# Half-height transpositions in pairs, into two neighbouring PSUM banks, in a two-block transformer kernel on one core

## The chip, the core and the metric

The kernel runs on one NeuronCore of a Trainium2 chip: TensorE (matrix products and transpositions), VectorE, ScalarE, GpSimd (POOL in the profile) and SyncE (SP), which issues the transfers. The metric is the device time of one execution in microseconds; lower is better.

## The reference, cut to what matters

Two blocks of two layers each over 256 positions of width 1024, batch 1, in float32. A layer of the first block projects x by `w_in`, runs three branches (retention with rotated queries and keys; chunk attention; differential attention with rotated queries and keys), merges them under gates, and ends in a feed-forward part:

```python
q = _rotary(q)                       # retention: 4 heads of 128
k = _rotary(k) * (dk ** -0.5)
...
q = _rotary(q) * (d ** -0.5)         # differential attention: 8 half heads of 64
k = _rotary(k)
...
merged = (g[:, :, 0] * jnp.einsum('bse,ed->bsd', o_a, w_branch_a[l])
          + g[:, :, 1] * jnp.einsum('bse,ed->bsd', o_b, w_branch_b[l])
          + g[:, :, 2] * jnp.einsum('bse,ed->bsd', o_c, w_branch_c[l]))
x = _layer_norm(DEEPNORM_ALPHA * x + mix, ln1_g[l], ln1_b[l])
u = jnp.einsum('bsd,df->bsf', x, w_ffn_in[l])
u_gate, u_up = jnp.split(u, 2, axis=-1)
ffn = jnp.einsum('bsf,fd->bsd', jax.nn.silu(u_gate) * u_up, w_ffn_out[l])
```

A layer of the second block is a feed-forward part, a mixer (convolution, gated MLP, sparse attention) and a second feed-forward part. So there are six feed-forward parts in all.

## The kernel before, in words

Every weight is brought in by SyncE in units of 128 x 2048 (`raw`), split by ScalarE into a rounded high part (`high`, L1857) and by VectorE into the low rest (`low`, L2096), both in `hl`. Each product is three matmuls, high by high, high by low, low by high (`mm3` L217 to L220, `mm3_onto` L223 to L227). TensorE needs the operand that is contracted with its positions along the free side, so results that come out with positions on the partitions are turned: `turn` (L1542) makes up to four 128 x 128 transpositions, one after the other, into one PSUM bank of 128 x 512; then ScalarE copies the bank out and, where high and low parts are wanted, VectorE subtracts.

The whole order is written out by a planner. `script` emits steps by name; each engine runs through the same list and does its part of every step in that order, so all five queues are in plan order. A step waits for semaphore counts of events that other engines' parts raise.

The eight PSUM banks are a ring, `PB` (class `Ring`, L186). `take` hands out the bank that was given back longest ago; `give` is called in the plan right after the steps that use the bank are added, and the next user's TensorE part waits for the event `free` that the last reader raises. Every bank carries a mark `dense`, set where its last use was a long projection or an accumulation. `take(True)` and `take(False)` prefer banks with or without that mark, plain `take()` goes by age alone (or by `spare`, where it is set). An accumulation holds its banks for long: a feed-forward part holds two from its third gate step and four from its fourth.

Steps that the change touches:
- `turn_split` (script L464, TensorE L1547, ScalarE L1860, VectorE L2099): the first x at the start (two steps of four blocks for each half of the rows; the steps that split the first weight unit, `lead`, stand between the two halves), the retention heads (`retention` L949, four blocks from a `tm` buffer), the differential attention (`da_attention` L1011, its `turn` makes two steps of four blocks one behind the other), and `gmlp`, which has a scale other than 1.
- `turn_copy` (TensorE L1554, ScalarE L1869): rotated queries and keys (`rot` L797, from an `rt` buffer, one step for each half of the rows, put off by one or two units), and the mask `gw` in `second_setup` L1089.
- `ffn_turn` (script L684, TensorE L1631, ScalarE L1918, VectorE L2183): in each feed-forward part (`ffn` L670) the first two hidden tiles come out with positions on the partitions and are turned, two blocks each. Both are put off by `P.later(1, ...)` and come out in one `tick`, one right behind the other.
- `ln_turn` (L1615), `weigh` (L1682) and the small transpositions of `stage_turn`, `pe_turn`, `gates_turn` and `cmp_gelu` (L1729 to L1782) are not touched.

Of the kernel before, what the change touches and what calls it, by code (L numbers as in the profile page):

```python
# [176 lines left out]
class Place:  # L177


    ring = None  # L180
# [5 lines left out]
class Ring:  # L186
# [5 lines left out]
    def take(self, dense=None):  # L192
# [259 lines left out]
def script(P):  # L452
# [11 lines left out]
    def turn_split(src, nk, dst, k0, src_events, before, i, out, scale=1.0, taken=()):  # L464

        for g in range(0, nk, 4):
            n = min(4, nk - g)
            b = PB.take()
            d = [dst[:, z, k0 + g:k0 + g + n, i * 128:(i + 1) * 128] for z in (0, 1)]
            last = g + 4 >= nk  # L470
            add("turn_split", b, [src[:, (g + k) * 128:(g + k + 1) * 128] for k in range(n)], src_events, taken if last else (),
                d, before, out(g, n), scale)
            PB.give(b)

# [322 lines left out]
    def rot(w, c0, nh, dh, dst, scale, name, before):  # L797
        yield from proj_n(w, c0)
        b = P.res
        for i in range(2):  # L800
            t1, t2 = RT.take(), TM.take()
            add("rotate", b[i], i, nh, dh, t1, t2)
            PB.give(b[i])
            TM.give(t2)

            def turn(i=i, t1=t1):
                tb = PB.take()
                add("turn_copy", tb, [t1.ap[:, k * 128:(k + 1) * 128] for k in range(4)], [t1.full], [t1.free],
                    dst[:, :, i * 128:(i + 1) * 128], before, [name + (i,)], scale)
                PB.give(tb)  # L810
                RT.give(t1)
            P.later(1 + i, turn)
        yield PART
# [60 lines left out]
    def first(l, o, now, nxt):  # L874
# [74 lines left out]
        def retention():  # L949
            def head(h):  # L950
# [10 lines left out]
                yield 1.3  # L961
                tb = PB.take()
                add("turn_split", tb, [tm.ap[:, i * 256 + c * 128:i * 256 + (c + 1) * 128] for c in range(2) for i in range(2)],
                    [tm.full], [tm.free], [O1[:, z, 2 * h:2 * h + 2, :] for z in (0, 1)], [P.o1_read], [("o1 ret", l)], 1.0)
                PB.give(tb)
                TM.give(tm)
# [122 lines left out]
    def second_setup(l, o):  # L1089
# [7 lines left out]
        for n, name in enumerate(("ck_w1_2", "cv_w1_2")):  # L1097
# [7 lines left out]
        yield 0.5  # L1105
        tb = PB.take()
        add("turn_copy", tb, [gw.ap[:, h * 128:(h + 1) * 128] for h in range(4)], [("gw masked", l)], [gw.free],
            m["wt"].rearrange("p (k t) -> p k t", k=4), [("wt read", l - 1)] if l else [("ca read", 1)], [("wt", l)], 1.0)
        PB.give(tb)
        RT.give(gw)  # L1110
# [310 lines left out]


class Signals:
    def __init__(self, sems, at):
# [107 lines left out]
def tensor_engine(e, P, steps, T, s):  # L1532
# [13 lines left out]

    def turn_split(b, blocks, events, taken, dst, before, out, scale):  # L1547
        e.wait_ge(*T["ident"])
        e.wait_ge(*T[b.before])
        for x in events:  # L1550
            e.wait_ge(*T[x])
        turn(b, blocks, *taken)

    def turn_copy(b, blocks, events, taken, dst, before, out, scale):  # L1554
        e.wait_ge(*T["ident"])
        e.wait_ge(*T[b.before])
        for x in events:
            e.wait_ge(*T[x])
        turn(b, blocks, *taken)

# [261 lines left out]
    def cmp_values(ob, l, et, first, last):  # L1822
# [4 lines left out]
        for c in range(2):  # L1827
# [3 lines left out]

    run(steps, dict(turn_split=turn_split, turn_copy=turn_copy, n_part=n_part, n_piece=n_piece, first_piece=first_piece, t_part=t_part,
                    ln_turn=ln_turn, out_piece=out_piece, ffn_turn=ffn_turn, ffn_down=ffn_down, score_pair=score_pair, score_parts=score_parts,
# [5 lines left out]
def scalar_engine(e, P, steps, T, s):  # L1839
# [19 lines left out]

    def turn_split(b, blocks, events, taken, dst, before, out, scale):  # L1860
        e.wait_ge(*T[b.full])
# [6 lines left out]

    def turn_copy(b, blocks, events, taken, dst, before, out, scale):  # L1869
        e.wait_ge(*T[b.full])  # L1870
        for x in before:
            e.wait_ge(*T[x])
        n = len(blocks)
        e.activation(dst, b.ap[:, 0:n * 128].rearrange("p (k t) -> p k t", k=n), ACT.Copy, scale=scale).then_inc(done.up(b.free, *out), 1)

# [42 lines left out]
    def ffn_turn(tb, tm, h, before, out):  # L1918
        e.wait_ge(*T[tb.full])
        e.wait_ge(*T[before])  # L1920
        e.activation(h[:, 0], tb.ap[:, 0:256], ACT.Copy).then_inc(done.up(("high",) + out), 1)

# [101 lines left out]
    run(steps, dict(start=start, lead_high=lead_high, high=high, turn_split=turn_split, o_split=turn_split, turn_copy=turn_copy, copy=copy, q_parts=q_parts, k_parts=k_parts, silu_gate=silu_gate, ln_split=ln_split,  # L2024
                    seed=seed, ffn_gate=ffn_gate, ffn_turn=ffn_turn, ffn_split=ffn_split, soft=soft, biased=biased,
# [44 lines left out]
def vector_engine(e, P, steps, T, s):  # L2070
# [27 lines left out]

    def turn_split(b, blocks, events, taken, dst, before, out, scale):  # L2099
# [367 lines left out]
    def cmp_turn(l, i, er, tb, et):  # L2467
# [4 lines left out]

    run(steps, dict(start=start, masks=masks, low=low, turn_split=turn_split, o_split=turn_split, scale=scale, rotate=rotate, silu_gate=silu_gate, ln_stats=ln_stats,
                    ln_norm=ln_norm, ln_split=ln_split, ln_last=ln_last, ffn_gate=ffn_gate, ffn_turn=ffn_turn,
# [87 lines left out]
```

## Time and profile before

| | |
|---|---|
| runs, median (lowest to highest) | 1980.91 us (1980.73 to 1981.51) |
| the profiled execution | 1980.39 us |
| its span in the trace | 1978.6 us |
| TensorE matmul, busy | 1966.6 us (99%), 13888 instructions |
| TensorE weight load, busy | 1801.2 us (91%) |
| VectorE, busy | 1248.4 us (63%) |
| ScalarE, busy | 911.8 us (46%) |
| GpSimd, busy | 98.6 us (5%) |
| TensorE's granted clock | 0.999 of full speed on average |

PE is TensorE's matmul, PEld its weight load, DVE VectorE, ACT ScalarE. A row of the time line is a run of like instructions: start in us from the start of the span, length, engine, line of the code, operation, output and input, `rows*columns` of the weights, shape of the moving operand, and how many. Matmuls overlap in the records, for each one's length holds its latency; what one costs is the distance from its start to the next one's. All transpositions of `turn` stand under L1544, with their data as the weights and the unit matrix (`cst`) moving.

### The profile page before, as it was taken

The page shows a single profiled execution, that of the slowest core. Times are in us where ns is not written, and L with a number is a line of the kernel's source. Part 1 is how long each engine was busy: PE and PEld are TensorE (multiplying, and loading weights), DVE is VectorE, ACT ScalarE, POOL GpSimd, SP SyncE. Part 2 cuts the span into 40 slices and gives each one's busy share as a digit, 9 for nine tenths or more (in the row PEclk, how much of TensorE's full clock was granted, in tenths as well). Part 3 has the DMA queues.
Part 4 walks back from the last instruction along what each step waited for, and adds up shares of the span by engine and source line. Part 5 has one row for each costly group of instructions (what it writes and reads, how often), then busy time and mean ns, then how long its engine had stood idle before and what let it go on. Part 6 is the DMA issues. An engine that isn't in the chain of part 4 may idle for free.

```text
span 1978.6 us, 31903 instructions
## 1 busy us (share of the span) xinstructions
PE 1966.6 (99%) x13888; PEld 1801.2 (91%) x13888; DVE 1248.4 (63%) x1759; ACT 911.8 (46%) x1217; POOL 98.6 (5%) x84
## 2 busy tenths in 40 slices
PE   8999999999999999999999999999999999999998
PEld 7889999999888999999999989899999998989997
DVE  6566666565756666655565567765556556776555
ACT  4445544444445555444354445544444444555442
POOL 0000001000100000100010020010010002001000
PEclk9999999999999999999999999999999999999999
DMA  7544566676454355696666656478666664646663
GB/s 282 189 143 140 180 204 197 198 209 192 170 170 149 133 187 192 196 262 180 184 209 185 186 168 171 108 201 258 183 179 204 186 188 150 192 114 197 186 186 106
DMA packets 421446, 361.85 MB, mean 183 GB/s; under 512 B 29425, under 2 KB 361529, under 8 KB 421305
## 3 DMA queue, kind: packets, MB, share of 16 engines
q1 hardware_dynamic: 421160, 359.74, 59.6%
q8 instruction: 109, 1.79, 0.4%
q14 instruction: 33, 0.26, 0.0%
q10 hardware_dynamic: 144, 0.07, 0.0%
HBM read 358.72 MB, written 1.05 MB: 182 GB/s over the span
## 4 chain that ended last, share of the span: by engine, by line
PE 99%; DVE 0%; DMA 0%; DVEq 0%; ACT 0%; issue 0%
PE ps L218 23%; PE ps L220 23%; PE ps L219 23%; PE ps L225 8%; PE ps L227 8%; PE ps L226 8%; PE ps L1544 3%; PE ps L1707 1%; PE ps L1655 1%; PE ps L1672 1%; PE ps L1745 0%; PE ps L1696 0%; PE ps L1813 0%; DMA cst<-in_const 0%; PE ps L1829 0%; PE ps L1723 0%
## 5 line engine op out<-in xcount | busy, mean ns | idle before, releaser
L2096 DVE TENSOR_TENSOR hl<-raw,hl 128x1024 fp32r<-128x1024 f32 (+2 forms) x535 | 722.2, 1383 | 382.0 <-ACT hl L1857 381.4
L218 PE MATMUL ps<-xt,hl 128*128 128x256 f32 (+1 forms) x2672 | 754.6, 282 | 0.0
L219 PE MATMUL ps<-xt,hl 128*128 128x256 f32 (+1 forms) x2672 | 746.2, 279 | 0.0
L220 PE MATMUL ps<-xt,hl 128*128 128x256 f32 (+1 forms) x2672 | 745.8, 279 | 0.0
L1857 ACT ACTIVATE hl<-raw 128x2048 fp32r<-128x2048 f32 (+1 forms) x338 | 613.7, 1824 | 218.6 <-PE ps L227 156.8
L218 PEld LDWEIGHTS ps<-xt,hl 128*128 128x128 f32 (+1 forms) x2672 | 500.9, 187 | 6.5 <-issue 3.1
L219 PEld LDWEIGHTS ps<-xt,hl 128*128 128x128 f32 (+1 forms) x2672 | 501.0, 188 | 3.1
L220 PEld LDWEIGHTS ps<-xt,hl 128*128 128x128 f32 (+1 forms) x2672 | 500.8, 187 | 0.2
L225 PE MATMUL ps<-hl,o 128*128 128x512 f32 x656 | 261.4, 398 | 0.0
L227 PE MATMUL ps<-hl,o 128*128 128x512 f32 x656 | 259.0, 395 | 0.0
L226 PE MATMUL ps<-hl,o 128*128 128x512 f32 x656 | 258.8, 394 | 0.0
L218 PE MATMUL ps<-hl,xt 128*128 128x512 f32 (+1 forms) x576 | 206.9, 359 | 0.5 <-DVE hl L2096 0.5
L1916 ACT ACTIVATE th<-ps 128x256 f32<-128x256 f32 x132 | 50.6, 384 | 328.8 <-PE ps L220 328.8
L220 PE MATMUL ps<-hl,xt 128*128 128x512 f32 (+1 forms) x576 | 202.1, 351 | 0.0
L219 PE MATMUL ps<-hl,xt 128*128 128x512 f32 (+1 forms) x576 | 202.1, 351 | 0.0
L227 PEld LDWEIGHTS ps<-hl,o 128*128 128x128 f32 x656 | 123.5, 188 | 28.9
L225 PEld LDWEIGHTS ps<-hl,o 128*128 128x128 f32 x656 | 123.5, 188 | 26.7 <-issue 0.8
L226 PEld LDWEIGHTS ps<-hl,o 128*128 128x128 f32 x656 | 123.7, 189 | 25.3
L218 PEld LDWEIGHTS ps<-hl,xt 128*128 128x128 f32 x576 | 108.4, 188 | 18.7 <-issue 1.7
L220 PEld LDWEIGHTS ps<-hl,xt 128*128 128x128 f32 x576 | 108.3, 188 | 15.9
L219 PEld LDWEIGHTS ps<-hl,xt 128*128 128x128 f32 x576 | 108.5, 188 | 14.5
L2179 DVE SCALAR_TENSOR_TENSOR tm<-th,ps 128x256 f32<-128x256 f32 x132 | 55.4, 420 | 98.9 <-ACT th L1916 94.8
(206 smaller groups left out, 1572.3 us busy)
## 6 DMA issues: line engine op xcount, KB each, us to landing
raw<-in_w_in SPq DMA_DIRECT2D x83, 1024.0 KB, 5.0
raw<-in_w_ffn_in SPq DMA_DIRECT2D x88, 512.0 KB, 5.1
raw<-in_ffn_gate SPq DMA_DIRECT2D x88, 512.0 KB, 3.9
raw<-in_ffn_up SPq DMA_DIRECT2D x88, 512.0 KB, 5.2
raw<-in_ffn_down SPq DMA_DIRECT2D x44, 1024.0 KB, 5.1
raw<-in_w_ffn_out SPq DMA_DIRECT2D x22, 1024.0 KB, 5.0
raw<-in_w_out SPq DMA_DIRECT2D x24, 512.0 KB, 4.6
raw<-in_w_branch_a SPq DMA_DIRECT2D x8, 1024.0 KB, 5.0
```

What stands on the lines that cost most here:

```text
L218: e.matmul(out, l[0], r[0], start=start, stop=False)
L219: e.matmul(out, l[0], r[1], start=False, stop=False)
L220: return e.matmul(out, l[1], r[0], start=False, stop=stop)
L225: e.matmul(out, l[0], r[0], start=False, stop=True, skip_group_check=True)
L226: e.matmul(out, l[0], r[1], start=False, stop=True, skip_group_check=True)
L227: return e.matmul(out, l[1], r[0], start=False, stop=True, skip_group_check=True)
L1544: ins = e.transpose(b.ap[:, k * 128:(k + 1) * 128], x, ident)
L1655: ins = e.matmul(b.ap[:, n * K:(n + 1) * K], qs[n][hh], ks[n][hh], start=n == 0, stop=mask is None and n == 1)
L1857: e.activation(m["hl"][:, k % NHL, 0, c], m["raw"][:, k % NRAW, c], ACT.Copy).then_inc(s.high.up(*([("high", k, h)] if parts == 2 else [(" ...
L1916: e.activation(tha, ga, ACT.Tanh, scale=0.5).then_inc(done.up(th.full), 1)
L2096: e.tensor_tensor(lo[:, c], m["raw"][:, k % NRAW, 0:n][:, c], hi[:, c].bitcast(F), ALU.subtract).then_inc(s.low.up(("low", k), *([("low", ...
L2179: e.scalar_tensor_tensor(tma, tha, 1.0, ga, ALU.add, ALU.mult).then_inc(done.up(th.free), 1)
```

## The change

Where a step turned blocks into one bank, it now takes two banks with neighbouring numbers (`Pair`, `neighbours`), and each block becomes two transpositions of 64 rows: the upper half's into the first bank, the lower half's into the second, 64 columns each. ScalarE and VectorE read both banks in one instruction through a view of four dimensions (`two_halves`). `turn_split` with scale 1, `turn_copy` and `ffn_turn` are changed; `turn_split` with another scale goes on as `turn_whole`.

```diff
+    def neighbours(self, dense=None):
+
+        dense = self.spare if dense is None else dense
+        age = {slot: n for n, slot in enumerate(self.order)}
+        pairs = [(dense is not None and (self.dense[x] != dense) + (self.dense[x + 1] != dense), max(age[x], age[x + 1]), x) for x in age if x + 1 in age]
+        x = min(pairs)[2]
+        return [self.at(slot) for slot in (x, x + 1)]
+
+    def at(self, slot):
+        self.order.remove(slot)
+        self.n += 1
+        u = Use(self, slot, self.n, self.latest[slot])
+        self.latest[slot] = u.free
+        return u
...
+class Pair:
+
+    def __init__(self, ring, psum, kind=False):
+        self.uses = ring.neighbours(kind)
+        a = self.uses[0].slot
+        self.ap = psum[:, a:a + 2, :]
+        self.before = [u.before for u in self.uses]
+        self.full, self.free = [u.full for u in self.uses], [u.free for u in self.uses]
...
-            b = PB.take()
+            b = Pair(PB, m["psum"]) if scale == 1.0 else PB.take()
...
-            PB.give(b)
+            PB.give(*(b.uses if scale == 1.0 else [b]))
...
                 def turn():
-                    tb = PB.take()
+                    tb = Pair(PB, m["psum"])
                     add("ffn_turn", tb, tm, h, free, ("ht", f, j))
-                    PB.give(tb)
+                    PB.give(*tb.uses)
...
+def two_halves(pair, dst, k0=0):
+
+    src = pair.ap[:, :, 64 * k0:64 * (k0 + dst.shape[1])].rearrange("p h (k t) -> p h k t", t=64)
+    return src, dst.rearrange("p k (h t) -> p h k t", h=2)
...
+    def turn_halves(pair, blocks, *events):
+        for k, x in enumerate(blocks):
+            for h in range(2):
+                rows = slice(64 * h, 64 * h + 64)
+                ins = e.transpose(pair.ap[:, h, k * 64:(k + 1) * 64], x[rows], ident[rows, rows])
+        ins.then_inc(done.up(*pair.full, *events), 1)
...
     def ffn_turn(tb, tm, h, before, out):
-        e.wait_ge(*T[tb.before])
+        for x in tb.before:
+            e.wait_ge(*T[x])
         e.wait_ge(*T[tm.full])
-        turn(tb, [tm.ap[:, i * 128:(i + 1) * 128] for i in (0, 1)], tm.free)
+        turn_halves(tb, [tm.ap[:, i * 128:(i + 1) * 128] for i in (0, 1)], tm.free)
...
     def ffn_turn(tb, tm, h, before, out):
         e.wait_ge(*T[("high",) + out])
-        e.tensor_tensor(h[:, 1], tb.ap[:, 0:256], h[:, 0].bitcast(F), ALU.subtract).then_inc(done.up(out, tb.free), 1)
+        (src, hi), (_, lo) = (two_halves(tb, blocks_of(h[:, z])) for z in (0, 1))
+        e.tensor_tensor(lo, src, hi.bitcast(F), ALU.subtract).then_inc(done.up(out, *tb.free), 1)
```

The other users of `turn_split` and `turn_copy` change in the same way: `Pair` in place of `PB.take()`, all of `tb.uses` given back, `turn_halves` in place of `turn`, `two_halves` in ScalarE's and VectorE's parts.

## Rows read from the trace of the kernel before

**Rows 1.** The page, part 1 (busy) and part 4 (chain by engine).
```profile
PE 1966.6 (99%) x13888; PEld 1801.2 (91%) x13888; DVE 1248.4 (63%) x1759; ACT 911.8 (46%) x1217; POOL 98.6 (5%) x84
...
PE 99%; DVE 0%; DMA 0%; DVEq 0%; ACT 0%; issue 0%
```

**Rows 2.** All waits of PE: who waited for whom, us in total, times, longest.
```profile
PE ps L1544 <- DMA cst<-in_const: 4.7, 1, 4.7
PE ps L218 <- DVE hl L2096: 0.5, 1, 0.5
```

**Rows 3.** Groups of instructions by line and form, L1544 on PE.
```profile
L1544 PE MATMUL ps<-cst,xs 128*128 128x128 f32 x160 | 22.8, 289 | 4.7 <-DMA cst<-in_const 4.7
...
L1544 PE MATMUL ps<-cst,rt 128*128 128x128 f32 x72 | 10.8, 272 | 0.0
L1544 PE MATMUL ps<-cst,tm 128*128 128x128 f32 x72 | 10.4, 272 | 0.0
```

**Rows 4.** Time line of PE, 91.6 to 92.8 us.
```profile
91.82 0.28 PE L219 MATMUL ps<-xt,hl 128*128 128x256 f32 x1
91.94 0.28 PE L220 MATMUL ps<-xt,hl 128*128 128x256 f32 x1
92.05 0.60 PE L1544 MATMUL ps<-cst,tm 128*128 128x128 f32 x4
...
92.61 0.28 PE L219 MATMUL ps<-xt,hl 128*128 128x256 f32 x1
```

**Rows 5.** Time line of PEld from 1220.3 us.
```profile
1220.52 0.14 PEld L1753 LDWEIGHTS ps<-cst,tm 30*128 30x128 f32 x2
```

**Rows 6.** Time line of PEld from 1246 us.
```profile
1246.57 0.97 PEld L1813 LDWEIGHTS ps<-small,q 64*128 64x128 f32 x16 [0.17 <-ACT th L1880]
```

**Rows 7.** Time line of PEld, 896.3 to 897.4 us.
```profile
896.71 0.13 PEld L1729 LDWEIGHTS ps<-cst,stage 12*128 12x128 f32 x1
896.77 0.14 PEld L1735 LDWEIGHTS ps<-cst,stage 32*128 32x128 f32 x1
896.83 0.14 PEld L1736 LDWEIGHTS ps<-cst,stage 32*128 32x128 f32 x1
```

**Rows 8.** Time line of PE, the same stretch.
```profile
896.51 0.27 PE L220 MATMUL ps<-xt,hl 128*128 128x256 f32 x1
...
897.35 0.39 PE L226 MATMUL ps<-hl,o 128*128 128x512 f32 x1
```

**Rows 9.** Time line of PEld, the start.
```profile
4.74 3.27 PEld L1544 LDWEIGHTS ps<-cst,xs 128*128 128x128 f32 x16 [4.74 <-DMA cst<-in_const]
```

**Rows 10.** Time line of DVE, 331 to 334.3 us, the first feed-forward part.
```profile
329.03 4.49 DVE L2096 TENSOR_TENSOR hl<-raw,hl 128x2048 fp32r<-128x2048 f32 x2 [1.97 <-ACT hl L1857]
333.44 0.75 DVE L2185 TENSOR_TENSOR o<-ps,o 128x256 fp32r<-128x256 f32 x2
```

**Rows 11.** Time line of PE, the same stretch.
```profile
331.23 0.60 PE L1544 MATMUL ps<-cst,tm 128*128 128x128 f32 x4
```

**Rows 12.** Time line of DVE, 237 to 243 us.
```profile
239.84 0.69 DVE L2107 TENSOR_TENSOR o<-ps,o 128x512 fp32r<-128x512 f32 x1 [0.31 <-ACT o L1867]
```

**Rows 13.** Time line of PE, 238.1 to 239.3 us.
```profile
238.29 1.03 PE L1544 MATMUL ps<-cst,tm 128*128 128x128 f32 x8
```

**Rows 14.** Time line of DVE, 109.6 to 113 us.
```profile
111.98 1.28 DVE L2107 TENSOR_TENSOR o<-ps,o 128x512 fp32r<-128x512 f32 x2
```

**Rows 15.** Time line of PE, 111.1 to 111.7 us.
```profile
111.28 0.60 PE L1544 MATMUL ps<-cst,tm 128*128 128x128 f32 x4
```

**Rows 16.** Time line of DVE, 157.9 to 160 us.
```profile
157.91 0.41 DVE L2121 TENSOR_TENSOR tm<-ps,cst 128x256 f32<-128x256 f32 x1
...
158.97 0.68 DVE L2212 COPY et<-ps 128x512 f32<-128x512 f32 x1
```

**Rows 17.** Time line of PE, 157.7 to 158.4 us.
```profile
157.91 0.60 PE L1544 MATMUL ps<-cst,rt 128*128 128x128 f32 x4
```

**Rows 18.** Busy time by stretch: us, PE, PEld, DVE, ACT, POOL, granted clock, DMA share, GB/s.
```profile
12.00:1974.00 1962.00, 1959.83 (x13860) 1795.42 (x13859) 1241.35 (x1747) 905.70 (x1208) 98.42 (x80) 1.00 0.60 182
```

More of the change, by code:

```diff
@@ L467, in turn_split @@
             n = min(4, nk - g)
-            b = PB.take()
+            b = Pair(PB, m["psum"]) if scale == 1.0 else PB.take()
             d = [dst[:, z, k0 + g:k0 + g + n, i * 128:(i + 1) * 128] for z in (0, 1)]
             last = g + 4 >= nk
-            add("turn_split", b, [src[:, (g + k) * 128:(g + k + 1) * 128] for k in range(n)], src_events, taken if last else (),
+            add("turn_split" if scale == 1.0 else "turn_whole", b, [src[:, (g + k) * 128:(g + k + 1) * 128] for k in range(n)], src_events, taken if last else (),
                 d, before, out(g, n), scale)
-            PB.give(b)
+            PB.give(*(b.uses if scale == 1.0 else [b]))
     def n_parts(w, r, c0, src, src_events, banks, first, last, after=()):
@@ L806, in turn @@
             def turn(i=i, t1=t1):
-                tb = PB.take()
+                tb = Pair(PB, m["psum"])
                 add("turn_copy", tb, [t1.ap[:, k * 128:(k + 1) * 128] for k in range(4)], [t1.full], [t1.free],
                     dst[:, :, i * 128:(i + 1) * 128], before, [name + (i,)], scale)
-                PB.give(tb)
+                PB.give(*tb.uses)
                 RT.give(t1)
@@ L961, in head @@
                 yield 1.3
-                tb = PB.take()
+                tb = Pair(PB, m["psum"])
                 add("turn_split", tb, [tm.ap[:, i * 256 + c * 128:i * 256 + (c + 1) * 128] for c in range(2) for i in range(2)],
                     [tm.full], [tm.free], [O1[:, z, 2 * h:2 * h + 2, :] for z in (0, 1)], [P.o1_read], [("o1 ret", l)], 1.0)
-                PB.give(tb)
+                PB.give(*tb.uses)
                 TM.give(tm)
@@ L1105, in second_setup @@
         yield 0.5
-        tb = PB.take()
+        tb = Pair(PB, m["psum"])
         add("turn_copy", tb, [gw.ap[:, h * 128:(h + 1) * 128] for h in range(4)], [("gw masked", l)], [gw.free],
             m["wt"].rearrange("p (k t) -> p k t", k=4), [("wt read", l - 1)] if l else [("ca read", 1)], [("wt", l)], 1.0)
-        PB.give(tb)
+        PB.give(*tb.uses)
         RT.give(gw)
@@ L1420, in quarter, with blocks_of @@
     return banks[c // 2].ap[:, 256 * (c % 2):256 * (c % 2) + 256].rearrange("p (k t) -> p k t", k=2)
+def two_halves(pair, dst, k0=0):
+    src = pair.ap[:, :, 64 * k0:64 * (k0 + dst.shape[1])].rearrange("p h (k t) -> p h k t", t=64)
+    return src, dst.rearrange("p k (h t) -> p h k t", h=2)
+def blocks_of(ap):
+    if len(ap.shape) == 2:
+        return ap.rearrange("p (k t) -> p k t", t=128)
+    return ap if ap.shape[2] == 128 else ap.rearrange("p k (m t) -> p (k m) t", t=128)
 class Signals:
@@ L1545, in turn, with turn_split, turn_whole @@
         ins.then_inc(done.up(b.full, *events), 1)
-    def turn_split(b, blocks, events, taken, dst, before, out, scale):
+    def turn_halves(pair, blocks, *events):
[4 more added lines that the diff above has]
+        ins.then_inc(done.up(*pair.full, *events), 1)
+    def turn_split(pair, blocks, events, taken, dst, before, out, scale):
         e.wait_ge(*T["ident"])
+        for x in pair.before + events:
+            e.wait_ge(*T[x])
+        turn_halves(pair, blocks, *taken)
+    def turn_whole(b, blocks, events, taken, dst, before, out, scale):
         e.wait_ge(*T[b.before])
@@ L1552, in turn_split, with turn_copy @@
         turn(b, blocks, *taken)
-    def turn_copy(b, blocks, events, taken, dst, before, out, scale):
+    def turn_copy(pair, blocks, events, taken, dst, before, out, scale):
         e.wait_ge(*T["ident"])
-        e.wait_ge(*T[b.before])
-        for x in events:
+        for x in pair.before + events:
             e.wait_ge(*T[x])
-        turn(b, blocks, *taken)
+        turn_halves(pair, blocks, *taken)
     def n_part(g, b, src, r, k0, i, src_events, first, last, after, seeded=False):
@@ L1631, in ffn_turn @@
     def ffn_turn(tb, tm, h, before, out):
-        e.wait_ge(*T[tb.before])
+        for x in tb.before:
+            e.wait_ge(*T[x])
         e.wait_ge(*T[tm.full])
-        turn(tb, [tm.ap[:, i * 128:(i + 1) * 128] for i in (0, 1)], tm.free)
+        turn_halves(tb, [tm.ap[:, i * 128:(i + 1) * 128] for i in (0, 1)], tm.free)
     def ffn_down(g, b, i, c, slots, h_events, events):
@@ L1830, in cmp_values @@
         ins.then_inc(done.up(ob.full, et.free, ("vb read", l), ("win read", l)), 1)
-    run(steps, dict(turn_split=turn_split, turn_copy=turn_copy, n_part=n_part, n_piece=n_piece, first_piece=first_piece, t_part=t_part,
+    run(steps, dict(turn_split=turn_split, turn_whole=turn_whole, turn_copy=turn_copy, n_part=n_part, n_piece=n_piece, first_piece=first_piece, t_part=t_part,
                     ln_turn=ln_turn, out_piece=out_piece, ffn_turn=ffn_turn, ffn_down=ffn_down, score_pair=score_pair, score_parts=score_parts,
@@ L1858, in high, with turn_split, o_split @@
             s.high.up(*([("high", k, h)] if parts == 2 else [("high", k, 0), ("high", k, 1)])), 1)
-    def turn_split(b, blocks, events, taken, dst, before, out, scale):
+    def turn_split(pair, blocks, events, taken, dst, before, out, scale):
+        e.wait_ge(*T[pair.full[1]])
+        for x in before:
+            e.wait_ge(*T[x])
+        src, d = two_halves(pair, blocks_of(dst[0]))
+        e.activation(d, src, ACT.Copy, scale=scale).then_inc(done.up(("split high", pair.full[1])), 1)
+    def o_split(b, blocks, events, taken, dst, before, out, scale):
         e.wait_ge(*T[b.full])
@@ L1867, in turn_split, with turn_copy @@
         e.activation(dst[0], src, ACT.Copy, scale=scale).then_inc(done.up(("split high", b.full)), 1)
-    def turn_copy(b, blocks, events, taken, dst, before, out, scale):
-        e.wait_ge(*T[b.full])
+    def turn_copy(pair, blocks, events, taken, dst, before, out, scale):
+        e.wait_ge(*T[pair.full[1]])
         for x in before:
             e.wait_ge(*T[x])
-        n = len(blocks)
-        e.activation(dst, b.ap[:, 0:n * 128].rearrange("p (k t) -> p k t", k=n), ACT.Copy, scale=scale).then_inc(done.up(b.free, *out), 1)
+        src, d = two_halves(pair, dst)
+        e.activation(d, src, ACT.Copy, scale=scale).then_inc(done.up(*pair.free, *out), 1)
     def copy(b, src, dst, scale, before, out):
@@ L1918, in ffn_turn @@
     def ffn_turn(tb, tm, h, before, out):
-        e.wait_ge(*T[tb.full])
+        e.wait_ge(*T[tb.full[1]])
         e.wait_ge(*T[before])
-        e.activation(h[:, 0], tb.ap[:, 0:256], ACT.Copy).then_inc(done.up(("high",) + out), 1)
+        src, d = two_halves(tb, blocks_of(h[:, 0]))
+        e.activation(d, src, ACT.Copy).then_inc(done.up(("high",) + out), 1)
     def ffn_split(tm, h, before, out):
@@ L2022, in cmp_exp @@
         e.activation(er.ap[:, 0:120], er.ap[:, 0:120], ACT.Exp).then_inc(done.up(("cmp exp", l, i)), 1)
-    run(steps, dict(start=start, lead_high=lead_high, high=high, turn_split=turn_split, o_split=turn_split, turn_copy=turn_copy, copy=copy, q_parts=q_parts, k_parts=k_parts, silu_gate=silu_gate, ln_split=ln_split,
+    run(steps, dict(start=start, lead_high=lead_high, high=high, turn_split=turn_split, o_split=o_split, turn_whole=o_split, turn_copy=turn_copy, copy=copy, q_parts=q_parts, k_parts=k_parts, silu_gate=silu_gate, ln_split=ln_split,
                     seed=seed, ffn_gate=ffn_gate, ffn_turn=ffn_turn, ffn_split=ffn_split, soft=soft, biased=biased,
@@ L2097, in low, with turn_split, o_split @@
             s.low.up(("low", k), *([("low", k, h)] if parts > 1 else [("low", k, 0), ("low", k, 1)])), 1)
-    def turn_split(b, blocks, events, taken, dst, before, out, scale):
+    def turn_split(pair, blocks, events, taken, dst, before, out, scale):
+        (src, hi), (_, lo) = (two_halves(pair, blocks_of(x)) for x in dst)
+        e.wait_ge(*T["split high", pair.full[1]])
+        low_part((hi, lo), src, scale).then_inc(done.up(*pair.free, *out), 1)
+    def o_split(b, blocks, events, taken, dst, before, out, scale):
         n = len(blocks) * 128
@@ L2471, in cmp_turn @@
                         ALU.mult).then_inc(done.up(et.full, tb.free), 1)
-    run(steps, dict(start=start, masks=masks, low=low, turn_split=turn_split, o_split=turn_split, scale=scale, rotate=rotate, silu_gate=silu_gate, ln_stats=ln_stats,
+    run(steps, dict(start=start, masks=masks, low=low, turn_split=turn_split, o_split=o_split, turn_whole=o_split, scale=scale, rotate=rotate, silu_gate=silu_gate, ln_stats=ln_stats,
                     ln_norm=ln_norm, ln_split=ln_split, ln_last=ln_last, ffn_gate=ffn_gate, ffn_turn=ffn_turn,
```

## The prediction

> **What bounds the kernel now.** I read the page's busy shares and its chain first: TensorE is busy 99% of the span and is the whole chain [rows 1]. Then its waits: in the whole span it stands still for the constant at the start and for 0.5 us after that, and for nothing else [rows 2]. So TensorE's own stream is the time. Whatever is added to it or taken from it moves the end one for one, and no later wait is there to absorb it. VectorE (63%) and ScalarE (46%) matter only where TensorE is made to wait for them. The span is 1978.6 us, the profiled execution 1980.39 us, the median of the runs 1980.91 us: 0.5 us lies between the last two, and I carry it over.
>
> **What is removed.** The diff touches 160 of the 480 transpositions at L1544: 16 of the first x, 72 from `rt`, 72 from `tm` [rows 3] (of the 160 from `xs`, 16 are the first x; the rest are `ln_turn`, which stays). The mean of 272 ns for one is latency; the cost is the pitch. Four of them cost this: the last matmul before starts at 91.94, the second one after at 92.61, which is 0.67 us; without them these two steps would be 2 x 0.117 = 0.23 (the pitch of L218 to L220 beside them). So a group of four costs 0.44 us, or 0.11 per block, with next to nothing at the edges [rows 4].
>
> **What is added on TensorE.** Each block becomes two instructions of 64 rows with 64 moving columns, in two banks. The trace has no 64-row transposition with 64 columns; the nearest rows are the small ones.
> Do the halves run beside each other? Two weight loads of 30-row transpositions at rows 0 and 32 stand in one row of 0.14 us, where one alone takes 0.13 [rows 5]; and 16 loads of 64 rows in alternating halves take 0.97 us, so a pair takes about 0.11 [rows 6]. I take it that pairs do overlap.
> How close do pairs follow? A transposition's weight load of 128 columns follows the one before by 0.06 us (896.71, 896.77, 896.83) [rows 7]; 64 moving columns are half of the 0.11 that 128 take, 0.05. So a pair costs 0.06, against 0.11 before. The bound above is the 0.11 of [rows 6], whose loads aren't transpositions; below it is the 0.05 of the moving columns. I take 0.06, since those rows are the same operation.
> What does leaving and entering cost? The three small transpositions of [rows 7] stand in a stream of full-height matmuls: from the last one before (896.51) to the second after (897.35) is 0.84 us, where 0.12 + 0.23 = 0.35 would do [rows 8]. They cost 0.49, of which 3 x 0.06 is their own. So 0.31 us is the price of going to fewer rows and coming back; the first load starts 0.20 after the matmul before it, where it otherwise runs ahead, and so does the load after the last. With 32 more moving columns in the last pair (0.03), four pairs cost 0.31 + 0.24 + 0.03 = 0.58 us against 0.44: 0.14 **more**. Two such groups in a row (eight blocks) cost 0.82 against 0.88.
> The Trainium skill speaks of this edge (TensorEngine Tiling (Array Packing), Key Properties): a change of the tiling mode drains TensorE, a change of tile alone doesn't. The trace agrees, with the 0.31 above. The skill also says (TensorE: Matmul & The Clock Gate, LDWEIGHTS) that a load costs by its columns, P/1.2, whatever its rows; for 128 columns that estimate is 107 ns a load, which [rows 7] contradict for transpositions with 0.06. What the higher pitch would do is worked out from [rows 6] among the rivals.
>
> **The sum of that.** The 160 blocks stand in 46 steps: 4 at the start, 16 in `rot`, 2 for `gw`, 8 in `retention`, 4 in `da_attention` (two directly after two), 12 in `ffn` (two blocks each, two steps in a row, so six runs of four). Two of the 16 in `rot` are followed by 64-row scores, whose own drain they take over: four pairs save 0.19 there, and nothing is added. So 14 + 2 + 8 + 6 = 30 runs x 0.14 = +4.2, two runs of eight x -0.06 = -0.1, two x -0.19 = -0.4: **+3.7 us**. At the start the sixteen have a pitch of 0.20 (3.27 us) [rows 9], and half the moving columns should halve it; the first L218 after them waits for VectorE [rows 2], which is fed by the first eight: the first x is split earlier by up to 8 x 0.1 = 0.8, and the lead copies on ScalarE stand behind that. **-0.6 us**, between 0 (if the lead's loads are late) and -0.9.
>
> **Banks, the larger term.** A pair takes two neighbours, and `neighbours` ranks by how many of the two were last used densely, before it looks at age. Banks that a pair gave back count as not dense. I stepped the list of free banks through the order of the takes and gives, with the new rule. In `ffn`, at the first of the two steps, five banks are free (before the first one 7, 5, 4, 6, 2, of which 7, 6 and 2 dense); 4 and 5 are taken, given back in the plan at once, and the second step finds 7, 6, 2, 4, 5 and takes **4 and 5 again**, for it is the only neighbouring pair without a dense bank. So the second transposition waits until VectorE has read the first result. Before, it had another bank. The same holds in all six `ffn`, and it is a wait of TensorE, with every projection queued behind it.
> Its length is in the trace of before. VectorE works through two `low` of L2096 until 333.52 and then does L2185, two in 0.75, so the first is done at about 333.86 [rows 10]. TensorE starts the second pair of blocks 0.22 after 331.23, at 331.45 [rows 11]. The wait is 2.4 us, six times: **14.5 us**.
> The same list gives the same clash elsewhere, in each of the two first layers: `da_attention`, second step, wants the banks that L2107 leaves at 239.84 + 0.69 = 240.53, when TensorE is at 238.29 + 0.43 = 238.72, 1.8 us [rows 12, 13]. `retention`, last head: free after the first L2107, 111.98 + 0.68, wanted at 111.28: 1.4 us [rows 14, 15]. `rot` for the keys of `da`, first half: its bank 6 was last a `weigh`, which L2212 reads until 158.97 + 0.68 = 159.65; wanted at 157.91: 1.7 us [rows 16, 17]. One `retention` head more comes 0.2 too early. Together 5.1 a layer, **10.2 us**. All other pairs find banks that have been free for over half a microsecond, and no other taker falls short. Each of the 14 waits ends in a load that nothing hides, and a semaphore: some 0.1 each (0.03 to 0.2), **+1.4 us**.
> Reading two banks in runs of 64 costs the readers nothing that I can see: L2121 reads 128 x 256 out of PSUM with a stride in 0.41, as L2185 does without [rows 10, 16]. If it cost 0.1, 14 waits would be 1.4 us longer. The ScalarE side has slack, it works ahead of VectorE. Nothing is moved on SP's or GpSimd's queue.
>
> Sum on the profiled execution: 1980.4 + 3.7 - 0.6 + 24.7 + 1.4 = 2009.6; plus 0.5 for the median: **2010 us**.
>
> **The rivals.**
> 1. Loads don't go faster for transpositions of half height, or the halves don't overlap: the pair costs 0.11, as in [rows 6]. 114 pairs (all but the first of each of the 46 steps) x 0.05 = +5.7, and the start gains nothing: 2016. For it: those are the only alternating 64-row loads with few columns. Against: [rows 7]. The page's rule for loads, above, would come to this rival. Chance 0.12.
> 2. The clock falls. Granted is 1.00, the 2.4 GHz level, from 12 to 1974 us [rows 18], and TensorE never stood still for over 0.5 us there. The first sixteen, right after 4.74 us of nothing, go at 0.20 instead of 0.11 a block [rows 9], as at the 1.2 GHz level. If the eight waits of 1.8 us and more did the same and cost some 2 us each: +16, 2026. Against: they are half as long. Chance 0.08. The Trainium skill (TensorE: Matmul & The Clock Gate, Part 1) lets the clock drop only after longer idling than these waits; no row of before shows that.
> 3. The banks come free in time (VectorE reads the pair ahead of its `low`, or the plan's order differs from my stepping): only the edges remain, 1980.9 + 3.7 - 0.6 = 1984. Against: the queues are in plan order and the `low` stands first. Chance 0.05.
> 4. **Faster**: going to 64 rows costs nothing for transpositions, and the banks are free. 144 blocks x 0.05 = -7.2, with -0.6: 1973. It decides at 0.17 us per edge pair; below that four pairs win. Against: 0.31 in [rows 8], themselves transpositions. Chance 0.02.
> That the diff doesn't do what it says I see no way for: 160 instructions more on TensorE are certain.
>
> **How the numbers follow.** The forecast has 0.71: its own range is 2004 to 2015 (pitch 0.05 to 0.07, waits shorter by what TensorE loses ahead of them, the start 0 to -0.9, readers +1.4). A last 0.02 goes to waits that are over half hidden, 1990 to 2000. With rivals 1 and half of 2 the range is 2000 to 2022. A measurement of this kernel can tell about 0.2% (4 us) from no change. Faster by that: rival 4 and nothing else, 0.02. Within: rival 3 (1984 is +0.16%), 0.05. Slower: 0.93.
>
> **What would show it.** In the profile after: 14048 matmuls; waits of TensorE's transpositions for VectorE's L2185-successor, six of about 2.4 us, in the chain too; eight more of 0.2 to 1.8; pairs of transpositions with starts a few ns apart and 0.06 from pair to pair; 0.2 before the first and about 0.2 after the last; the clock still 1.00. If TensorE's waits stay under 2 us in total, the stepping of the banks is wrong. If single waits exceed 3 us, ScalarE or VectorE fell behind as well.

## The result and the profile after

| | before | after |
|---|---|---|
| runs, median (lowest to highest) | 1981.11 us (1980.73 to 1981.58) | 2018.21 us (2013.75 to 2019.49) |
| the profiled execution | 1980.39 us | 2019.49 us |
| its span in the trace | 1978.6 us | 2017.7 us |
| mean granted clock of that execution | 0.999 | 0.994 |

The change made the kernel slower: ratio 1.0183, 95% interval 1.0172 to 1.0194, five runs each (the 1980.91 us of the forecast was the median of the first three of before). The forecast was 2010 us, with a range of 2000 to 2022. It said +29 us; the medians are 37.1 us apart, the spans of the two profiled executions 39.1 us. The direction and the banks were seen rightly; about 10 us came from something that the forecast had set at nothing.

The busy line and the chain by engine (the page of after), which answer to [rows 1]:

```profile
PE 1981.8 (98%) x14048; PEld 1806.0 (90%) x14048; DVE 1251.3 (62%) x1759; ACT 914.6 (45%) x1217; POOL 98.6 (5%) x84
...
PE 92%; DVE 5%; ACT 2%; issue 0%; DMA 0%; POOL 0%; DVEq 0%
```

VectorE was 0% of the chain and is now 5%. All waits of TensorE in after, the view of [rows 2] (who waited for whom, us in total, times, longest). L1588 is the half-height transposition; L2248 is `ffn_turn` on VectorE, L2169 the subtraction of `turn_split`, L2275 VectorE's copy in `weigh`, L2153 `low`:

```profile
PE ps L1588 <- DVE o L2248: 13.8, 6, 2.3
PE ps L1588 <- DVE o L2169: 5.8, 4, 1.7
PE ps L1588 <- DMA xs<-in_x: 5.0, 1, 5.0
PE ps L1588 <- DVE et L2275: 3.3, 2, 1.7
PE ps L233 <- DVE hl L2153: 1.1, 1, 1.1
```

Six waits of 2.3 us in the feed-forward parts and six of 1.13 to 1.75 elsewhere are 22.9 us. What one of the six is made of stands in the chain of after between 338 and 344 us (start, length, what):

```profile
338.17 4.49 DVE hl L2153 x2
342.67 0.34 DVE o L2248
...
343.06 0.35 PE ps L1588 x4
```

It is the forecast's story: two `low` of 2.2 us each stand ahead of the step that reads the bank, and TensorE stands until that is read. The same place on TensorE in after (start, length, engine, line, operation, tiles, weights, moving operand, how many):

```profile
340.20 0.27 PE L235 MATMUL ps<-xt,hl 128*128 128x256 f32 x1
340.41 0.34 PE L1588 MATMUL ps<-cst,tm 64*128 64x64 f32 x4
343.06 0.35 PE L1588 MATMUL ps<-cst,tm 64*128 64x64 f32 x4 [2.31 <-DVE o L2248]
343.34 0.58 PE L233 MATMUL ps<-xt,hl 128*128 128x256 f32 x1
...
344.57 0.41 PE L235 MATMUL ps<-xt,hl 128*128 128x256 f32 x1
344.78 0.41 PE L233 MATMUL ps<-xt,hl 128*128 128x256 f32 x1
```

Before the wait such products follow each other by 0.117 us, after it by 0.21. That is the part which the forecast lacked. Stretches of after with the granted clock (from:to and its length, busy time with instructions of PE, PEld, DVE, ACT and POOL, then the clock, the DMA share and GB/s):

```profile
247.70:251.10 3.40, 3.40 (x19) 3.40 (x18) 2.33 (x3) 1.44 (x1) 0.00 (x0) 0.50 0.59 228
343.30:346.70 3.40, 3.40 (x20) 3.36 (x17) 1.60 (x4) 2.25 (x6) 0.00 (x0) 0.51 1.08 341
843.35:846.80 3.45, 1.14 (x11) 1.08 (x12) 2.60 (x4) 1.04 (x3) 0.00 (x0) 1.00 0.61 178
1036.20:1039.60 3.40, 3.10 (x16) 2.99 (x17) 1.84 (x5) 1.59 (x5) 0.00 (x0) 0.50 1.16 337
```

A clock of 0.5 is the 1.2 GHz level. Three more such stretches follow, at 1343.4, 1534.5 and 1841.7 us. So the clock fell six times, five times at a wait of 2.3 us and once at one of 1.75. It didn't fall at a fixed distance from the wait: at 1036.2 us TensorE still stood for another 0.3 us (the wait ended at 1036.49), at 343.3 the wait had ended 0.2 us before, and at 247.7 it had ended 1.4 us before, with 1.4 us of work in between. The third line shows the 2.3 us wait (843.35 to 845.66 us) that it did not fall after. In before it stays at the 2.4 GHz level from 12 to 1974 us [rows 18]. One fall costs what is lost at half speed: 3.4 us x (1 - 0.117 / 0.213) = 1.5 us; the later matmuls of after, held against the same matmuls of before, move by 1.55 to 1.65 us over each stretch. Six falls are some 9.7 us.

The whole move of that execution then adds up. Of 39.1 us, 22.9 are the waits, 9.7 the falls, 1.2 the start (below), and 5.3 are left for the edges and restarts at 46 steps.

### The profile page after: what moved, and what is told of

Same layout as the page of the kernel before. It is cut to its first block, busy times and chain, and to the rows that moved or that the text cites. A ratio compares the mean times of both kernels' runs of the same rounds, so it can differ in the third digit from the quotient of the medians.

```text
span 2017.7 us, 32221 instructions
## 1 busy us (share of the span) xinstructions
PE 1981.8 (98%) x14048; PEld 1806.0 (90%) x14048; DVE 1251.3 (62%) x1759; ACT 914.6 (45%) x1217; POOL 98.6 (5%) x84
## 4 chain that ended last, share of the span: by engine, by line
PE 92%; DVE 5%; ACT 2%; issue 0%; DMA 0%; POOL 0%; DVEq 0%
PE ps L233 22%; PE ps L235 21%; PE ps L234 21%; PE ps L240 8%; PE ps L242 8%; PE ps L241 8%; DVE hl L2153 2%; PE ps L1581 2%; ACT hl L1906 1%; PE ps L1756 1%; PE ps L1588 1%; PE ps L1721 1%; PE ps L1704 0%; DVE small L2264 0%; PE ps L1794 0%
## 5 line engine op out<-in xcount | busy, mean ns | idle before, releaser
L2153 DVE TENSOR_TENSOR hl<-raw,hl 128x1024 fp32r<-128x1024 f32 (+2 forms) x535 | 723.4, 1384 | 399.1 <-ACT hl L1906 398.5
```

Source lines behind the costliest of these rows:

```text
L2153: e.tensor_tensor(lo[:, c], m["raw"][:, k % NRAW, 0:n][:, c], hi[:, c].bitcast(F), ALU.subtract).then_inc(s.low.up(("low", k), *([("low", ...
```

## The experiments

All ran for one core, each with runs of the kernel before on the same chip: its median there was 1980.81 us for the first four and 1980.78 us for the last four. Two theories stood at the outset. **Theory A**: the time went to the waits for banks, and the clock fell because TensorE stood still; the halves themselves cost only their edges. **Theory B**: the halves or the two-bank reads cost more themselves, and bring the falls about.

**1. Feed-forward turns share a pair.** Both turns of a feed-forward part write different columns of one pair, and the readers wait for both:

```diff
-                    tb = Pair(PB, m["psum"])
+                    if j == 0:
+                        shared.append(Pair(PB, m["psum"]))
+                    tb = shared[0].part(2 * j)
...
-                    PB.give(*tb.uses)
+                    if j == 1:
+                        PB.give(*tb.uses)
```

> The changed kernel, but in each feed-forward part the two turns use different columns of one pair of banks, so that the second no longer waits for the first to be read (readers wait for both). Theory (waits for banks, and clock falls that follow the waits): six waits of 2.5 us and five clock falls of 1.7 us go: 2018.2 - 15.0 - 8.5 = 1995 us, with at most one stretch at half clock left, after the differential attention. Rival (the clock falls because of the half-height transpositions themselves): only the waits go, 2003 us, and five or more half-clock stretches stay.

Measured: 1996.65 us (1994.77 to 1997.14), ratio 1.0078, interval 1.0063 to 1.0093. The waits of the feed-forward parts are gone from TensorE's list, the others are as they were (waits of this kernel, then its one stretch at the lower clock):

```profile
PE ps L1602 <- DVE o L2183: 5.8, 4, 1.7
PE ps L1602 <- DVE et L2289: 3.3, 2, 1.6
```
```profile
746.80:750.30 3.50, 3.50 (x19) 3.50 (x18) 2.44 (x3) 1.25 (x1) 0.00 (x0) 0.51 0.52 202
```

The medians of this kernel and of after are 21.6 us apart: 13.8 us of waits and five falls fewer (8 us) make 21.8. The falls left with the waits, while the halves stayed.

**2. No pair that was just given back.** Experiment 1, and the search for a pair looks first at whether a bank is one of the last two given back:

```diff
+        late = self.order[-2:]
-        pairs = [(dense is not None and (self.dense[x] != dense) + (self.dense[x + 1] != dense), ...
+        pairs = [((x in late) + (x + 1 in late), (self.dense[x] != dense) + (self.dense[x + 1] != dense), ...
```

> As e1, and the pair is chosen by a rule that avoids the two banks given back last, so that nearly no pair has to wait (0.8 us in all by the free list). What is left is the price of the edges, 0.13 to 0.14 us a group as read from the two traces (3.4 us in all), the start (1.2 us), and no clock falls: 1986.5 us. Rival (half-height transpositions lower the clock): 1992 or more, with half-clock stretches. Rival (the edges were really part of the waits): 1982.

Measured: 1986.54 us (1986.06 to 1987.4), ratio 1.0029, interval 1.0018 to 1.004. TensorE's waits, with the one for the constant left out:

```profile
...
PE ps L235 <- DVE hl L2168: 1.2, 1, 1.2
PE ps L1603 <- DVE tm L2198: 0.7, 2, 0.4
```

The clock falls nowhere in TensorE's work. Against the trace of before the end moves by 5.9 us: 0.8 at the start, 0.9 in the two small waits with their restarts, and 4.2 at the edges. That is the price of the halves themselves, and they have no gain to set against it. The other 31.7 us of the change (1986.54 to 2018.21) came from the choice of banks.

**3. After's pairs, but full height.** The order of takes and gives stays; the transposition is that of before and writes the first bank only, and the readers read that one alone:

```diff
-            for h in range(2):
-                rows = slice(64 * h, 64 * h + 64)
-                ins = e.transpose(pair.ap[:, h, k * 64:(k + 1) * 64], x[rows], ident[rows, rows])
+            ins = e.transpose(pair.ap[:, 0, k * 128:(k + 1) * 128], x, ident)
...
```

> The changed kernel's pairs of banks and its waits, but each block is turned whole, 128 rows, into the first bank of the pair; the second bank is held and unused. Theory: waits (22.9 us) and clock falls stay, edges (3.4 us) and the slow start (1.2 us) go: 2013.5 us. Rival (the clock falls because of the half-height transpositions): no half-clock stretches, 2004 us.

Measured: 2012.81 us (2009.29 to 2014.85), ratio 1.0159, interval 1.0144 to 1.0174. The waits of the feed-forward parts, and one of this kernel's four stretches at the lower clock (the others start at 1339.0, 1530.2 and 1837.4 us):

```profile
PE ps L1585 <- DVE o L2245: 14.0, 6, 2.4
```
```profile
1031.80:1035.20 3.40, 3.34 (x16) 3.35 (x17) 1.60 (x5) 1.62 (x5) 0.00 (x0) 0.50 1.15 340
```

Theory B falls: with no half-height instruction and no two-bank read in the kernel, it is 32 us slower than before, and the clock falls as in after. Together with experiment 2 this shows that the wait brings the fall. The halves' own price comes out smaller here than in experiment 2: after ends 4.7 us later than this kernel in the traces, 3.2 us of that are its two falls more, and 1.5 us are left. At the eight groups in `rot` that no wait follows after takes 0.14 to 0.16 us longer; where a wait stands, part of the edge comes off the wait (in `retention` 1.13 us in after against 1.26 and 1.27 here).

**4. Halves not alternated.** Experiment 2, with all upper halves of a group first and then all lower ones:

```diff
-        for k, x in enumerate(blocks):
-            for h in range(2):
+        for h in range(2):
+            for k, x in enumerate(blocks):
```

> As e2, but a group first turns the upper halves of all its blocks and then the lower ones, so that neighbours in the stream use the same 64 rows. Theory (halves overlap only when they alternate; a pair costs 0.06 us, one after the other 0.12): 160 x 0.06 = 9.6 us over e2, 1996 us. Rival (TensorE overlaps them in any order, or never did): the time of e2.

Measured: 1986.97 us (1986.33 to 1987.55), ratio 1.0031, interval 1.0019 to 1.0042: experiment 2's time. My theory, that the halves overlap only when one of each follows the other, fell. The first `rt` group of after on TensorE, and then the same group of this kernel:

```profile
26.77 0.39 PE L235 MATMUL ps<-hl,xt 128*128 128x512 f32 x1
27.08 0.46 PE L1588 MATMUL ps<-cst,rt 64*128 64x64 f32 x8
...
27.81 0.39 PE L234 MATMUL ps<-hl,xt 128*128 128x512 f32 x1
```
```profile
26.89 0.40 PE L237 MATMUL ps<-hl,xt 128*128 128x512 f32 x1
27.22 0.47 PE L1603 MATMUL ps<-cst,rt 64*128 64x64 f32 x8
...
27.96 0.39 PE L236 MATMUL ps<-hl,xt 128*128 128x512 f32 x1
```

From the last product before the group to the second one after it (the first is not shown) there are 1.04 us in after and 1.07 here. Within the group the loads of a pair start 3 ns apart in after and 12 ns apart here, and the pairs follow each other by 0.06 us in both, although here four loads of the upper rows were issued ahead of the first of the lower rows.

**5. The start at full height.** Experiment 2, with the first x turned as in before:

```diff
+            halved = scale == 1.0 and dst is not XT
-            b = Pair(PB, m["psum"]) if scale == 1.0 else PB.take()
+            b = Pair(PB, m["psum"]) if halved else PB.take()
...
```

> As e2, but the first x is turned whole, 128 rows into one bank, as before; half-height pairs everywhere else. Theory (the start loses because the clock comes up late in these runs whatever the transpositions are; the halves themselves save 0.4 us there, by the first product's start in e2 and e3): 1986.9 us, 0.4 over e2. Rival (it is the half-height transpositions at the start that hold the clock down): 1985.3 us, and the clock up by 8.1 us as in the kernel before.

Measured: 1988.69 us (1986.86 to 1989.5), ratio 1.0038, interval 1.0024 to 1.0051. The time doesn't answer what the run was made for. The start takes other banks, the list stands in another order from there on, and one clash came back (a wait of TensorE, and the clock just after it):

```profile
PE ps L1604 <- DVE o L2186: 1.8, 1, 1.8
```
```profile
243.60:247.00 3.40, 3.40 (x18) 3.40 (x18) 2.30 (x4) 1.76 (x1) 0.00 (x0) 0.50 0.68 264
```

Without that wait and fall (1.8 + 1.6 us) it would be near 1985.3, the rival's number. That is worked out, not measured, and the hit is partly luck: against the trace of experiment 2 the start gives 0.56 us, and a small wait that is absent here 0.48. The trace of the start does speak for the rival. The products of 512 columns go at the full pace from the first one on, which starts at 9.06 us:

```profile
9.37 0.39 PE L236 MATMUL ps<-hl,xt 128*128 128x512 f32 x1
9.60 0.39 PE L237 MATMUL ps<-hl,xt 128*128 128x512 f32 x1
```

The run also shows how brittle a fixed list is: four steps changed at the start, and a wait appears 240 us later.

**6. The upper rows twice.** Experiment 2, with both transpositions of a pair reading rows 0 to 63. The lower halves of the turned blocks are left out:

```diff
-                ins = e.transpose(pair.ap[:, h, k * 64:(k + 1) * 64], x[rows], ident[rows, rows])
+                ins = e.transpose(pair.ap[:, h, k * 64:(k + 1) * 64], x[0:64], ident[0:64, 0:64])
```

> As e2, but both transpositions of a pair read rows 0 to 63, so nothing in a group uses the other half of the rows (the lower halves are left out; the output isn't the reference's). Theory (two streams overlap because they use different rows, in whatever order they are issued): loads follow at 0.06 us each, a pair costs 0.12, 160 x 0.06 = 9.6 us over e2: 1996 us. Rival (TensorE issues any two of them together): the time of e2.

Measured: 1993.87 us (1993.34 to 1994.79), ratio 1.0065, interval 1.0052 to 1.0079. The same group on TensorE in this kernel:

```profile
28.35 0.40 PE L237 MATMUL ps<-hl,xt 128*128 128x512 f32 x1
28.67 0.71 PE L1603 MATMUL ps<-cst,rt 64*128 64x64 f32 x8
...
29.66 0.40 PE L236 MATMUL ps<-hl,xt 128*128 128x512 f32 x1
```

1.31 us instead of 1.04, so 0.07 more per pair than in after; against experiment 2 a group of four takes 0.24 to 0.25 us more, 0.06 per pair. The overlap is real and needs different rows: with it a pair costs 0.06 us, without it 0.12. The 36 groups' worth of blocks behind the start times 0.24 is 8.6 us, less 0.9 for experiment 2's two small waits, which are absent here: 7.7. The two medians are 7.3 us apart. The sum is no closer than a microsecond or two, for the starts of the two profiled runs differ by 1.95 us besides.

**7. Only where eight blocks stand together.** The kernel before, with half-height pairs in one place, the groups of eight in the sparse attention of the second block (`weigh`), which the change had left alone. One pair of banks holds all eight:

```diff
+        if P.both and PB.spare is None:
+            pair = Pair(PB, m["psum"])
+            for n in range(2):
+                er, et = ers[n], ET.take()
+                add("weigh_pair", pair, n, [er.ap[:, k * 128:k * 128 + 128] for k in range(4)], er, ...)
...
+            PB.give(*pair.uses)
```

> The kernel before, with half-height pairs only in eight groups of eight blocks in the second block's sparse attention (turned weights), where one pair of banks holds both results and no bank is taken besides. Theory (a group costs 0.34 + 0.06 a block against 0.11 a block; two groups are followed by 64-row scores whose drain is there anyway): 6 x -0.06 and 2 x -0.4 = -1.1 us, 1980.0 us, no new waits. Rival (the two readers' wait for both halves reaches the values): +0.5 us a group, 1985.

Measured: 1979.84 us (1979.52 to 1980.52, 11 runs), ratio 0.9995, interval 0.9986 to 1.0004. One of its two groups that 64-row scores follow, in before and then in this kernel:

```profile
1245.48 0.28 PE L220 MATMUL ps<-xt,hl 128*128 128x256 f32 x1
1245.61 1.03 PE L1544 MATMUL ps<-cst,er 128*128 128x128 f32 x8
1246.57 1.07 PE L1813 MATMUL ps<-small,q 64*128 64x15 f32 x16
1247.57 0.38 PE L218 MATMUL ps<-xt,hl 128*128 128x256 f32 x1
```
```profile
1245.71 0.28 PE L238 MATMUL ps<-xt,hl 128*128 128x256 f32 x1
1245.92 0.71 PE L1721 MATMUL ps<-cst,er 64*128 64x64 f32 x16
1246.46 1.02 PE L1850 MATMUL ps<-small,q 64*128 64x15 f32 x16
1247.41 0.38 PE L236 MATMUL ps<-xt,hl 128*128 128x256 f32 x1
```

From the product before to the product after there are 2.09 us in before and 1.70 here. So where the work behind is at 64 rows anyway, eight pairs do gain, 0.38 to 0.39 us at each of two groups, and the other six gain 0.03 to 0.04 each. That sums to 1 us in 1980, which the interval can't tell from nothing. No wait was added.

**8. The kernel before again**, for a second trace of its start.

> The kernel before, unchanged, for a second profile of its start. Theory (when the clock comes up at the start varies from run to run): up anywhere from 8 to 13 us, span between 1978.5 and 1980. Rival (8.1 us belongs to the kernel before): 8.1 us again.

Measured: 1981.29 us, span 1979.5. Its start on TensorE, and then that of after (the profile's clock column doesn't show this first stretch, so it is read from the distances of the products):

```profile
4.93 3.65 PE L1544 MATMUL ps<-cst,xs 128*128 128x128 f32 x16 [4.93 <-DMA xs<-in_x]
8.97 0.76 PE L218 MATMUL ps<-hl,xt 128*128 128x512 f32 x1 [0.40 <-DVE hl L2096]
...
10.67 0.40 PE L219 MATMUL ps<-hl,xt 128*128 128x512 f32 x1
10.91 0.40 PE L220 MATMUL ps<-hl,xt 128*128 128x512 f32 x1
```
```profile
5.04 2.34 PE L1588 MATMUL ps<-cst,xs 64*128 64x64 f32 x32 [5.04 <-DMA xs<-in_x]
8.43 0.77 PE L233 MATMUL ps<-hl,xt 128*128 128x512 f32 x1 [1.06 <-DVE hl L2153]
...
11.98 0.48 PE L235 MATMUL ps<-hl,xt 128*128 128x512 f32 x1
12.30 0.40 PE L233 MATMUL ps<-hl,xt 128*128 128x512 f32 x1
```

Products of 512 columns follow by 0.43 us at first and by 0.23 later. The change of pace came at about 10.5 us here and at 8.1 in the first trace of before. With the first x turned at full height it came at 11.2, 8.1 and 9.5 us in experiments 3, 5 and 7; with halves at the start at 12.2 in after and at 13.0, 11.5, 12.6 and 14.9 in experiments 1, 2, 4 and 6. So it varies by 3 us within each kind, and the two kinds don't overlap: the five starts at full height lie between 8.1 and 11.2, the five with halves between 11.5 and 14.9, with one trace of each run.

## Why the prediction was right, and where it was wrong

**Banks.** Right, and by the steps given. The stepping of the free list named six clashes in the feed-forward parts and three larger ones in each of the two first layers; the waits came there and nowhere else. The six were put at 2.4 us and measured 2.3. `da_attention` 1.8, measured 1.75; `rot` 1.7, measured 1.65; `retention` 1.4, measured 1.13. The two of 0.2 us did not show. In sum 24.7 us forecast, 22.9 measured: TensorE came a little later to each, and that took the difference off the wait.

**Edges and restarts.** 3.7 + 1.4 = 5.1 us forecast, 5.3 left over in the sum above. A group of four takes 1.04 us in after, where before took 0.91 (25.59 to 26.50): +0.13, with 0.14 forecast from three small transpositions of 12 and 32 rows [rows 7, 8]. The split between the two terms is less exact than their sum: experiment 2 puts the edges alone at 4.2 us, which leaves 1.1 for the restarts. The reader of two banks takes 0.42 us (L2248), as with one (L2185), so that it costs nothing was right too. A feed-forward part moves TensorE by 2.65 us in all, wait, restart and edge; the steps gave 2.4 + 0.1 + 0.14 = 2.64.

**Overlap.** Right in the number, 0.06 us per pair; experiment 6 shows that it comes from the different rows. Rival 1 (0.11) is out. So is the Trainium skill's rule that it leaned on (TensorE: Matmul & The Clock Gate, LDWEIGHTS): with 107 ns a load, an estimate by that rule, loads on the same rows could not follow each other by 0.06 us, and in experiment 6 they do (eight loads of L1603 in 0.58 us, each 0.14 long).

**The start.** The step that put it at -0.6 us failed, and it measured +1.2 (profiled execution of after against that of before). The first product did start 0.38 us earlier, within the forecast's 0 to -0.9. What the step didn't see is that the products behind it run at half pace until the clock rises, and that this came at 12.2 us in after, behind 3.7 us of products, where in before it came ahead of the first product. Part of the +1.2 is chance: experiment 3, at full height, has +1.2 as well. At the product that starts at 20 us in before, the four other starts at full height stand 0.2 to 1.2 us later, and after and experiments 1, 2 and 4 stand 0.8 to 1.6 us later; the means differ by some 0.75 us, which is an estimate of what the halves themselves cost there instead of their gain. The clock's rise was later in every trace with halves than in any without (experiment 8). Why halves would delay it no run shows.

**The clock.** This is the step that missed most. The forecast had it as rival 2, with +2 us for each of eight waits and a chance of 0.08, and set it at nothing in its own sum. It came on top of the forecast: six falls of 1.6 us. The reason given against it, that the waits are half as long as the 4.74 us at the start, was no evidence that a shorter stop is harmless: within TensorE's work the trace of before had no stop between 0.5 and 4.7 us. Behind that work it had one, which [rows 18] leave out by ending at 1974 us. TensorE's last matmul of before ends at 1971.83 us, and 2.3 us later the clock is down (same columns as above):

```profile
1971.90:1974.10 2.20, 0.00 (x0) 0.00 (x0) 2.03 (x5) 0.00 (x0) 0.54 (x1) 1.00 0.11 42
1974.20:1978.50 4.30, 0.00 (x0) 0.00 (x0) 1.72 (x3) 0.00 (x0) 0.00 (x0) 0.50 0.33 122
```

So a stop as long as six of the forecast waits was followed by the lower clock in before itself, and the cost should have stood between 0 and the start's doubled pace at all eight waits. The Trainium skill (TensorE: Matmul & The Clock Gate, Part 1) lets the clock drop only after longer idling than these waits. Here the trace disagrees: it fell at waits of 1.75 and 2.3 us. The measurement decides. In the same unit, the forecast's 29.2 us plus 9.7 for the falls and 1.8 for the start is 40.7, less the 1.8 us that the waits were shorter: 38.9, against 39.1.

**The spread.** After's runs lie 5.7 us apart, those of before 0.9. They order by the granted clock: 2013.75 us at 0.997, 2017.14 at 0.996, 2018.21 at 0.995, 2018.31 and 2019.49 at 0.994. From 0.997 to 0.994 is 0.003 x 2018 = 6 us of clock lost, and the times differ by as much. That fits runs which differ by how many of their waits the clock fell at; it isn't shown, for one of the five has a trace.

**Left open.** Why one wait of 2.3 us brings a fall and another doesn't. In the profiled runs of after and experiment 3 nine of twelve waits of 2.3 to 2.4 us did; of the seven between 1.7 and 1.85 us in after and experiments 1, 3 and 5 three did; of the twelve from 1.1 to 1.65 us in after and experiments 1 and 3 none did. The length of the wait doesn't tell them apart, and in `ffn` the work around them is the same. What does differ is the moment: the clock changed from 0.3 us before the end of the wait (after, 1036.2 us) to 1.7 us behind it (experiment 1, 746.8 against 745.15 us), so the moments at which it changes aren't tied to the wait, and where a wait lies to them may decide. No run here was made to test that. Pairs of banks that aren't neighbours were not tried.

## What to carry to other kernels

When a change makes a step take two buffers where it took one, step the free list by hand through the steps around it: who gives a buffer back in the plan right before the next step wants one, and what stands in the reader's queue ahead of that read. On TensorE a wait is not over when it ends. Of the 19 waits of 1.7 to 2.4 us in these traces 12 brought a stretch at half speed that costs another 1.6 us, so price such waits with both and let the range reach that far. If the profile of before has no stop of that length within the work, see what the clock does behind the last matmul. Half-height pairs pay some 0.3 us for going down and coming back against 0.05 saved per block: four blocks lose 0.14 us, eight gain 0.04, and only next to work that is at 64 rows already do eight gain 0.38.

## What was not expected of the hardware

- TensorE's granted clock fell to 0.50 at standstills of 1.75 to 2.4 us, for 3.4 us each time; it came down between 0.3 us before the end of the standstill and 1.7 us behind it, in the latter case after that much work at full pace.
- Two 64-row transpositions in different halves of the rows run together (0.06 us a pair) even when four loads for one half were issued ahead of the first for the other: 1.07 us for the group against 1.04. Both on the same rows cost 0.12 us.
- The pace of the first products changes at 8.1 to 14.9 us after the start of the span, twice at different moments (8.1 and 10.5 us) in one and the same kernel; in the five traces with halves at the start it changed later (11.5 to 14.9 us) than in the five at full height (8.1 to 11.2).
